# The causal mask of an attention stage moved from VectorE into TensorE's accumulation

## What is computed

```python
# FOX (8 heads): forgetting attention, c = cumsum(log f)
logits = einsum('bqhd,bkhd->bhqk', qb, k) * scale + (cb[..., :, None] - c[..., None, :])
p = softmax(where(k_pos <= q_pos, logits, NEG_INF)); out = p @ v
# CMP: 15 compressed keys per group, masked by cmp_end <= q_pos
pc = softmax(where(mc, lc, NEG_INF)) * mc
# SLC, WIN: selected blocks and window; with 256 tokens both cover every causal key
ps = softmax(where(tok <= q_pos, ls, NEG_INF)); pw = softmax(where(mw, lw, NEG_INF))
o = g0 * (pc @ v_cmp) + g1 * (ps @ v_sel) + g2 * (pw @ v_win)
```

## Time and profile before

| | value |
|---|---|
| median of 3 runs | 2330.33 us (2324.06 to 2330.75) |
| the profiled execution's own time | 2327.65 us, span 2325.9 us |
| granted TensorE clock, mean | 0.831 |
| busy share of the span: PE, DVE, ACT, POOL | 75%, 33%, 19%, 12% |
| the attention stage | 179.28 to 259.73 us of the span: 80.45 us |

### The profile page before, as it was taken

The page is one execution under the profiler, slowest core; times in us unless marked ns, Lnnn a source line. Parts: engine busy times, 40 slices in busy tenths (PEclk is TensorE's granted clock), DMA queues, the critical chain, the costliest instruction groups (busy, mean ns, idle before and its releaser), DMA issues. The chain is left out here.

```text
span 2325.9 us, 22733 instructions
## 1 busy us (share of the span) xinstructions
PE 1733.6 (75%) x8678; PEld 871.0 (37%) x8678; DVE 756.1 (33%) x1643; ACT 438.6 (19%) x915; POOL 288.9 (12%) x297
## 2 busy tenths in 40 slices
PE   6997887987877778859788867666666666666675
PEld 6975687433333333329687631111111111111111
DVE  3425327876767666543464220000000000000001
ACT  4414223222212222224411020000000000000000
POOL 0000002433343333400051000000000000000000
PEclk9987998999899998989888777777777777787777
DMA  5530248999999999965000369999999999999996
GB/s 205 179 132 17 73 138 330 420 420 420 420 420 420 420 420 420 420 256 211 1 1 1 127 253 420 420 421 420 421 420 421 420 421 420 420 420 420 421 420 273
DMA packets 111080, 738.63 MB, mean 318 GB/s; under 512 B 13856, under 2 KB 15136, under 8 KB 27040
## 3 DMA queue, kind: packets, MB, share of 16 engines
q1 hardware_dynamic: 73856, 469.14, 50.0%
q0 software_dynamic: 36864, 268.45, 27.8%
q10 hardware_dynamic: 288, 0.08, 0.0%
HBM read 736.58 MB, written 1.05 MB: 317 GB/s over the span
## 5 line engine op out<-in xcount | busy, mean ns | idle before, releaser
L886 PE MATMUL ps<-arena 128*128 128x512 f32 x768 | 390.1, 661 | 132.0 <-ACT arena L947 132.0
L1898 PE MATMUL ps<-arena,xe 128*32 128x512 f32 x2048 | 353.7, 792 | 169.0 <-DMA arena<-in_experts_in 168.8
L1944 DVE TENSOR_TENSOR low<-low,ps 128x512 f32<-128x512 f32 x16 | 11.0, 687 | 890.4 <-PE ps L1898 890.4
L886 PEld LDWEIGHTS ps<-arena 128*128 128x128 f32 x768 | 156.0, 209 | 357.6 <-issue 188.6
L1030 DVE CUSTOM_DVE_ANT_0 arena<-arena,ps 128x1024 f32<-128x1024 f32 x192 | 231.9, 1218 | 113.5 <-DMA arena<-in_peer,arena 109.0
L833 POOL DMA_INDIRECT arena<-in_peer,arena x192 | 182.0, 948 | 692.8 <-DVE arena L1022 364.7
L1912 PE MATMUL ps<-arena,hT 128*32 128x512 f32 x1024 | 182.0, 811 | 102.2 <-DMA arena<-in_experts_down 90.5
L1898 PEld LDWEIGHTS ps<-arena,xe 128*32 128x32 f32 x2048 | 50.5, 122 | 461.7 <-DMA arena<-in_experts_in 419.6
L1912 PEld LDWEIGHTS ps<-arena,hT 128*32 128x32 f32 x1024 | 26.2, 127 | 240.5 <-DMA arena<-in_experts_down 213.3
L947 ACT ACTIVATE arena<-ident,arena 128x128 f32<-128x128 f32 x256 | 81.8, 390 | 122.1 <-DVE arena L1039 120.6
L333 PE MATMUL ps<-first_h_parts,first_w_parts 128*128 128x256 f32 x816 | 100.3, 286 | 5.3 <-DVE first_h_parts L298 4.3
(11 more groups left out here) (352 smaller groups left out, 1984.1 us busy)
## 6 DMA issues: line engine op xcount, KB each, us to landing
arena<-in_experts_in SPq DMA_DIRECT2D x256, 1024.0 KB, 26.9
arena<-in_experts_down SPq DMA_DIRECT2D x128, 1024.0 KB, 26.9
ring<-in_stream SPq DMA_DIRECT2D x80, 512.0 KB, 3.5
arena<-in_stream SPq DMA_DIRECT2D x14, 1024.0 KB, 7.5
arena<-in_peer,arena POOLq DMA_INDIRECT x192, 27.1
h<-in_x SPq DMA_DIRECT2D x1, 1024.0 KB, 5.1
arena<-in_sel SPq DMA_DIRECT2D x1, 1024.0 KB, 5.7
arena<-in_subkeys SPq DMA_DIRECT2D x2, 512.0 KB, 5.0
```

The lines of the kernel that those rows point to most:

```text
L886: last = nc.tensor.matmul(ps[:, 4 + 2 * t + half, :], diag[:, n % DIAGS, :], slot(n)[:, D + half * BANK:D + (half + 1) * BANK], start=firs ...
L1898: last = nc.tensor.matmul(ps[32 * j:32 * (j + 1), 4 + r // KB, :], xe[:, k, :], w[:, j * BANK:(j + 1) * BANK], start=(k == 0), stop=(k == ...
```

## The change

TensorE adds the mask: after the matmuls of a pair of heads it multiplies the identity by the mask and accumulates onto the same PSUM columns, two more fp32 matmuls for each pair of heads, four for each unit (64 in all). For FOX, SLC and WIN they cover only the 128 keys of the diagonal block, for CMP all 15. VectorE's addition into `lg` is gone; the maximum is taken from PSUM, and the exponentials read PSUM and write `lg`. `score(n)` now waits for the four exponentials of unit n-2, and the wait for a free `lg` buffer moves from DVE to ACT.

```diff
--- before.py
+++ after.py
@@ -559,12 +559,11 @@
     lg = T.carve(LB, 4, S)
     stat = T.sb(stack, "stat", [P, LB, 4, 4])
     pT = T.carve(2, 4, 2, P)
-    masked, max_ready, exp_done, p_ready = (sem(n) for n in ("att_masked", "att_max", "att_exp", "att_p"))
+    max_ready, exp_done, p_ready = (sem(n) for n in ("att_max", "att_exp", "att_p"))
     scores, pt_ps, pt_sb, values_done, out_sb = (sem(n) for n in ("att_scores", "att_pt_ps", "att_pt_sb", "att_values", "att_out_sb"))
     units = [(t, hg, kind) for t in range(NT) for hg in range(2) for kind in (FOX, CMP, SLC, WIN)]
     sc = lambda n: ps[:, 2 * (n % 2):2 * (n % 2) + 2, :].rearrange("p a (b s) -> p a b s", b=2)
     width = lambda t, kind: NCMP if kind == CMP else P * (t + 1)
-    quad = lambda ap: ap.rearrange("p (a b) s -> p a b s", a=2)
 
     def stages(*parts):
 
@@ -580,7 +579,7 @@
                 t, hg, kind = units[n]
                 w = width(t, kind)
                 if n >= 2:
-                    pe.wait_ge(masked, n - 1)
+                    pe.wait_ge(exp_done, 4 * (n - 1))
                 rows = slice(t * P, (t + 1) * P)
                 for hp in range(2):
                     pair = 2 * hg + hp
@@ -591,11 +590,16 @@
                         for par, half, hd, dst in halves:
                             nc.tensor.matmul(dst, clog[half, 0, rows], sel8[half, hd, 0:w], start=False, stop=False)
                         for par, half, hd, dst in halves:
-                            last = nc.tensor.matmul(dst, sel8[half, hd, 0:P], clog[half, 1, 0:w], start=False, stop=True)
+                            nc.tensor.matmul(dst, sel8[half, hd, 0:P], clog[half, 1, 0:w], start=False, stop=False)
                     else:
                         for par, half, hd, dst in halves:
                             k = {CMP: kcmp[half, hg, 0:NCMP], SLC: proj[half, KSL + hg, 0:w], WIN: proj[half, KWN + hg, 0:w]}[kind]
-                            last = nc.tensor.matmul(dst, proj[half, NQ + pair, rows], k, start=True, stop=True)
+                            nc.tensor.matmul(dst, proj[half, NQ + pair, rows], k, start=True, stop=False)
+                    for par, half, hd, dst in halves:
+                        if kind == CMP:
+                            last = nc.tensor.matmul(dst, T.ident[:, :], mask_cmp[:, 0, t, 0:w], start=False, stop=True)
+                        else:
+                            last = nc.tensor.matmul(dst[:, w - P:w], T.ident[:, :], causal[:, P:2 * P], start=False, stop=True)
                 last.then_inc(scores, 1)
 
             def transposes(n):
@@ -639,21 +643,11 @@
         def _(dve):
             link = T.link(dve, "dve", T.chain_dve)
 
-            def mask_max(n):
+            def maximum(n):
                 t, hg, kind = units[n]
                 w = width(t, kind)
                 dve.wait_ge(scores, n + 1)
-                if n >= LB:
-                    dve.wait_ge(pt_ps, n - LB + 1)
-                if kind == CMP:
-                    m = mask_cmp[:, 0, t, 0:w]
-                else:
-                    m = causal[:, S - w:S]
-                x = lg[:, n % LB, :, 0:w]
-                nc.vector.tensor_tensor(quad(x), sc(n)[:, :, :, 0:w],
-                                        m.unsqueeze(1).unsqueeze(1).broadcast_to([P, 2, 2, w]), ALU.add).then_inc(masked, 1)
-                dve.wait_ge(masked, n + 1)
-                link(nc.vector.reduce_max(stat[:, n % LB, 0, :], x, AX.X))
+                link(nc.vector.reduce_max(stat[:, n % LB, 0, :].rearrange("p (a b) -> p a b", a=2), sc(n)[:, :, :, 0:w], AX.X))
                 nc.vector.tensor_scalar(stat[:, n % LB, 1, :], stat[:, n % LB, 0, :], -SCALE, None, ALU.mult).then_inc(max_ready, 1)
 
             def normalise(n):
@@ -671,7 +665,7 @@
                     link(nc.vector.tensor_tensor(x, x, m, ALU.mult))
                 nc.vector.tensor_tensor(x, x, stat[:, n % LB, 3, :].unsqueeze(2).broadcast_to([P, 4, w]), ALU.mult).then_inc(p_ready, 1)
 
-            stages(mask_max, normalise)
+            stages(maximum, normalise)
 
         @block.scalar
         def _(act):
@@ -679,9 +673,10 @@
                 t, hg, kind = units[n]
                 w = width(t, kind)
                 act.wait_ge(max_ready, n + 1)
+                if n >= LB:
+                    act.wait_ge(pt_ps, n - LB + 1)
                 for q in range(4):
-                    x = lg[:, n % LB, q, 0:w]
-                    nc.scalar.activation(x, x, ACT.Exp, bias=stat[:, n % LB, 1, q:q + 1], scale=SCALE,
+                    nc.scalar.activation(lg[:, n % LB, q, 0:w], sc(n)[:, q // 2, q % 2, 0:w], ACT.Exp, bias=stat[:, n % LB, 1, q:q + 1], scale=SCALE,
                                          accum_out=stat[:, n % LB, 2, q:q + 1]).then_inc(exp_done, 1)
 
             def evacuate(n):
```

## The result

The changed kernel takes 2333.82 us (median of 20 runs, 2329.5 to 2340.05), the kernel before 2325.31 (20 runs on the same chips, 2322.81 to 2330.75). The ratio is 1.0034, with a 95% interval of 1.0026 to 1.0041: 8 us slower, 6.0 to 9.5. The median of three runs that the forecast started from, 2330.33, was 5 us high. The profiled execution of the changed kernel took 2333.73 us (span 2331.9).

What follows compares the result with a forecast made beforehand. Attention was taken as bound by a chain over PE, DVE and ACT through the even units. 31.15 us of DVE and ACT plus PE's work and odd masks gave a 76.8 us stage, 3.6 less: 2326.7 us, range 2317 to 2338.

Steps and rivals of the forecast that it cites:

- Switching between half-row and full-row matmuls: Changes around TensorE's masks: taken as 0, bounds 0 and some 0.1 us at each of four changes, 3 us in all.
- the forecast's own sum: Attention stage = 31.15 + 32.5 (1 + c) + 5 (0.9 (1 + c) - 0.87), giving 76.8 us at c = 0.35.
- c: Share of TensorE's work on the chain done at half clock: 0.58 before the change, taken as 0.35 after.
- The mask addition leaves DVE: Eight even-unit additions leave the chain, four of 0.72 and four of 1.26 us: 7.9 us saved; odd ones worth nothing.
- The maximum reads PSUM: DVE's maximum on the chain: 0.06 us less for each of eight, 0.5 us saved.
- The exponentials read PSUM: ACT's exponentials on the chain: 0.028 us less each, 0.9 us saved; bounds 0 and 0.9.
- The new wait: Scores of unit n waiting for exponentials of unit n-2: only unit 2 moves, cost about 0.
- The clock: TensorE in attention: masks fill its waits, so c falls from 0.58 to 0.35, midway to 0.13 at 7% idle.
- Odd units' masks: Hidden by TensorE's wait for the evacuation; what sticks out is 5 x (0.9 (1 + c) - 0.87) us.
- Rival 2: TensorE's masks done at half clock: slower, deciding from c = 0.64 with a stage of 87.6 us, +7; chance 0.11.
- Rival 3: Loop moves to odd units, TensorE always busy: 58.3 us of work, stage 78 us, kernel 2327.7; chance 0.10.
- What would show it wrong: Stage clock still 0.75 or less, a mask much over 0.225 us, or TensorE waiting for `att_exp` in mid-stage.

Runs made afterwards that it cites:

- the wait alone: Kernel before, with only the scores of unit n made to wait for the exponentials of unit n-2: 2329.61 us against 2326.42, ratio 1.0007.
- The odd zeros: Kernel before plus 32 TensorE matmuls adding zeros to the scores of the odd units, DVE still masking: 2327.07 us against 2326.94, ratio 0.9998.
- the DVE version: Changed kernel without mask matmuls; DVE adds the mask in place in PSUM on the diagonal block: 2322.03 us against 2326.94 for the kernel before, 0.9985.
- half-row masks: Changed kernel, each full-row mask matmul replaced by two with half the rows, masks partly left out: 2324.34 us against 2327.56 for the kernel before, 0.9989.
- zeros everywhere: Kernel before plus 64 TensorE matmuls adding zeros in the places of the masks, DVE still masking: 2343.10 us against 2326.42, ratio 1.0066.

## Why the prediction was wrong

**The step that failed** is "Switching between half-row and full-row matmuls is in no row; ... I take 0". It measured 0.49 us for a unit at full clock and 0.77 at half clock, on top of the 0.9 and 1.7 us for the columns. Even the upper bound, "some 0.1 us at each of four changes", is below that; going in costs 0.10 each time, coming out 0.30. The reason given, that matmuls of different shapes follow each other with PE busy in the rows of the stretches, proves nothing: PE is shown busy through a change too. The loss is in the distance between starts, and there the trace of the kernel before had it, 0.53 us in place of 0.43 (unit 12, above).

With the measured terms the forecast's own sum gives the result. DVE and ACT on the chain: 31.15, plus 0.5 for the saving of the maximum that did not come, less 0.4 for the exponentials, 31.3. PE without masks: 25.3 x 1.41 = 35.7. Masks, 0.41 of them at half clock: 0.59 x 1.39 + 0.41 x 2.47 = 1.83 a unit, 14.7 for the even units. Odd units: 5 x (1.83 - 0.87) = 4.8. Together 86.5 us, against 85.7 and 86.6 measured. With the forecast's price, 0.9 x 1.41 = 1.27, the masks are 4.5 us less on the even units and 2.8 less on the odd ones, 7.3 together. The rest of the miss of 8.9 us is the clock, c = 0.41 for 0.35, worth 2.2 us; together they are 0.6 us too much, within the scatter of a stage. The sum puts 55 us on PE and 31.3 on DVE and ACT, the stretches show 56.2 and 29.5.

Point by point:

- *The mask addition leaves DVE*: right in kind. DVE's busy time fell by 11.9 us, and the stage without masks is 12.5 us shorter, a part of it by a higher clock.
- *The maximum reads PSUM*: the saving of 0.06 us each did not come. It takes 1224 ns from PSUM and 1.22 us from SBUF; the small pair in the earlier trace rows did not carry over.
- *The exponentials read PSUM*: 0.16 us for a unit instead of 0.11.
- *The new wait*: right, about 0, shown by the wait alone. In the changed kernel it does not show at all, because unit 2's scores stand behind unit 1's masks on PE until 186.47.
- *The clock*: c came out as 0.41 for 0.35, near it by luck. "PE idles for 27% of the stage" was the lever, on a straight line to full clock, with 7% idle to give c = 0.13. PE did idle for 7% (6.2 of 85.7 us), and c was 0.41. The odd zeros took idleness from 27% to 14% and the clock of the stage stayed where it was; the DVE version idles for 27% and has 0.82. The line is refuted, and the 0.35 was the middle between it and today's clock.
- *Odd units' masks*: the cover was there, as the zeros in odd units show. The masks were longer than it.
- *Rival 2* had the right sign, from c = 0.64 up; c was 0.41, so it is not what happened. *Rival 3* came nearest in kind: PE is busy 93% of the stage and has become the bound. It priced that at 43.9 + 14.4 = 58.3 us of work at full clock. The 43.9, busy time times the stage's mean clock, was too high (40.4 while PE is busy), and the 14.4 too low (21.0); there were 61.4.
- *What would show it wrong*: "if a mask costs much over 0.225 us at full clock" was the one that came true: 1.39 / 4 = 0.35 with its share of the changes.

**What stays open.** The stages differ by 5.3 and 4.6 us, the medians by 8.5. The profiled executions as a whole differ by less, 6.0 and 3.5 us of span: the one of the kernel before took 2327.65, 2.3 above the median of 20 runs. Behind the stage the four profiles of the two kernels have 2066.2 to 2068.2 us each, so some 3 us of the difference between the medians are not placed. What sets the granted clock within the stage was not found: while PE is busy it was 0.69 before, 0.77 in the changed kernel, 0.82 with the same masks ahead of the scores and 0.83 with half-row masks.

## What to carry to other kernels

A matmul that uses all 128 rows, put among matmuls of 64 rows, costs more than its columns: put such matmuls together, or give them the same rows as their neighbours. Look for this loss in the distance between the starts of instructions, as the busy time does not show it. Work moved to an engine that seems to have 27% idle is hidden only where the wait lies that it fills: 32 added matmuls cost nothing in one half of the units and 13.5 us in the other, and adding the mask in place on the diagonal alone was better than moving it.

## What the runs showed of the hardware

- *The price of changing rows*, fp32 matmuls of 128 columns: 0.10 us into full rows and 0.30 out (0.19 and 0.11) at clock 1.00, 0.18 and 0.47 at 0.50. Half-row records follow each other every 0.056 us and full-row ones every 0.11, with durations of 0.39 and 0.71 for four. This fits two half-row matmuls, on different rows, overlapping; whether they do was not tried.
- *The granted clock is no function of how busy PE is.* For the stage it was 0.75 at 87% busy (zeros everywhere), 0.74 at 86% (odd zeros), 0.82 at 73% (mask on DVE), 0.85 at 88% (half rows), 0.79 at 93% (the changed kernel). Counted only while PE is busy it was 0.75, 0.72, 0.76, 0.83 and 0.77, and 0.69 before, at 73% busy. Nor do the same matmuls bring the same clock: the changed kernel's first 12.34 us are all busy and all at 0.50, in both of its profiles, while the kernel with zeros everywhere, which has matmuls of the same shapes in the same order there, left 0.50 after 5.3 us (second fence):

```profile
178.00:190.34 12.34, 12.34 (x66) 10.62 (x67) 2.02 (x6) 3.88 (x17) 0.00 (x0) 0.50 0.00 1
```

```profile
177.78:183.10 5.32, 5.32 (x32) 4.56 (x32) 0.00 (x0) 1.24 (x1) 0.00 (x0) 0.50 0.00 0
183.10:186.50 3.40, 3.40 (x29) 2.80 (x28) 2.15 (x6) 1.50 (x8) 0.00 (x0) 0.96 0.02 5
```

- *A DVE reduction from PSUM costs what one from SBUF costs*: 1224 ns at 1024 elements and 692 at 512 from PSUM, means of 1220 and 686 from SBUF in the kernel before. The Trainium skill (VectorE: DVE Perf Modes, The TRN2 errata) gives a PSUM source 62 cycles more than an SBUF source; the measurement does not show it. An addition in place in PSUM took 698 ns, against 688 from PSUM to SBUF.
